# Scoring a sample's cached keys on TensorE from pages the host has laid out in columns

## What is computed

```python
p   = x @ w_in                       # q | k | v | q_m | B | C | h, 2560 columns, for 264 tokens
# prompt: 8 heads of causal attention and 4 heads over 256 memory tokens
# sample b, head h, over its 2048 cached keys in 8 blocks of 256:
gate   = q . mean(k over block)      # one value for each block
chosen = top_k(gate, 3)              # the other five blocks get no weight
logits = q . k / 8 - slope_h * distance
probs  = softmax(logits over the chosen blocks and the token's own key)
o      = probs @ v                   # over the 2048 cached values and the own one
x1  = layernorm(alpha * x + mix(o_attention, o_conv, o_memory) @ w_out)
y   = layernorm(alpha * x1 + moe(x1))   # top 4 of 32 experts, 12.6 MB of weights each
```

## Time and profile before

| | |
|---|---|
| median of 3 runs | 1324.86 us |
| profiled execution, its own time | 1325.73 us |
| its span in the trace | 1323.9 us |
| TensorE busy | 1030.6 us, 78% |
| VectorE busy | 531.0 us, 40% |
| DMA moved | 499.13 MB, mean 377 GB/s |
| chain that ended last | DMA 43%, PE 39%, DVE 6% |

### The profile page before, as it was taken

One profiled execution on the slowest core, in us unless ns is written; L12 is line 12 of the kernel. 1 busy time (PEld: TensorE's weight loads), 2 busy tenths in 40 slices (PEclk: granted clock), 3 DMA queues, 4 the chain that ended last, 5 costly groups with the idle time before them and its releaser, 6 DMA issues.

```text
span 1323.9 us, 20019 instructions
## 1 busy us (share of the span) xinstructions
PE 1030.6 (78%) x7278; PEld 399.6 (30%) x7279; DVE 531.0 (40%) x953; ACT 228.9 (17%) x504; POOL 152.3 (12%) x136
## 2 busy tenths in 40 slices
PE   7998678977985999855556659975778975868956
PEld 5776343433231333211012113221212321222313
DVE  1699884358432444421112123422414441223414
ACT  1212451222111112100010111110111110101112
POOL 2576722205200000000000000000000000000000
PEclk9999678987998999987677779987989997979978
DMA  9986998988999938899999999799999799999993
GB/s 364 398 315 254 358 366 299 391 367 327 370 422 422 422 123 340 346 423 422 423 421 423 421 423 422 318 422 421 423 421 422 318 420 423 421 423 421 423 422 123
DMA packets 72404, 499.13 MB, mean 377 GB/s; under 512 B 7357, under 2 KB 7930, under 8 KB 19034
## 3 DMA queue, kind: packets, MB, share of 16 engines
q1 hardware_dynamic: 66336, 429.88, 79.0%
q0 software_dynamic: 4688, 67.26, 12.6%
q10 hardware_dynamic: 1354, 1.65, 0.3%
HBM read 496.06 MB, written 2.71 MB: 377 GB/s over the span
## 4 chain that ended last, share of the span: by engine, by line
DMA 43%; PE 39%; DVE 6%; issue 4%; POOL 3%; SPq 3%; ACT 1%; ACTq 0%; DVEq 0%; POOLq 0%
DMA gate_up_w<-in_w_gate_up 28%; PE bank L921 14%; DMA down_w<-in_w_down 11%; PE bank L970 10%; PE bank L577 2%; PE bank L705 2%; PE bank L982 2%; DVE down_w L1552 2%; PE bank L794 2%; SPq L505 1%; DMA ring_b<-in_cache_v,page_row 1%; DMA ring_b<-in_cache_k,page_row 1%; PE bank L893 1%; DMA ring_a<-in_cache_k,page_row 1%; POOL ring_b L1487 1%
## 5 line engine op out<-in xcount | busy, mean ns | idle before, releaser
L921 PE MATMUL bank<-gate_up_w,ring_b 128*32 128x512 f32 x3264 | 449.1, 657 | 207.8 <-DMA gate_up_w<-in_w_gate_up 207.7
L1897 DVE TENSOR_TENSOR ring_b<-bank,work 32x512 f32<-32x512 f32 x100 | 68.4, 684 | 486.4 <-ACT work L1268 484.8
L921 PEld LDWEIGHTS bank<-gate_up_w,ring_b 128*32 128x32 f32 x3264 | 89.3, 114 | 454.2 <-DMA gate_up_w<-in_w_gate_up 303.9
L970 PE MATMUL bank<-down_w,ring_b 128*32 128x512 f32 x1632 | 190.2, 598 | 16.9 <-DMA down_w<-in_w_down 16.9
L1494 POOL TENSOR_TENSOR gate_up_w<-gate_up_w,ring_a 128x1024 f32<-128x1024 f32 x1 | 2.3, 2344 | 973.8 <-ACT gate_up_w L1314 973.8
L1268 ACT ACTIVATE work<-bank 32x512 f32<-32x512 f32 x100 | 58.8, 588 | 242.1 <-PE bank L970 240.8
L970 PEld LDWEIGHTS bank<-down_w,ring_b 128*32 128x32 f32 x1632 | 51.2, 111 | 152.1 <-issue 115.8
L1922 DVE TENSOR_SCALAR ring_b<-bank 128x256 f32<-128x256 f32 x51 | 21.7, 425 | 158.3 <-PE bank L921 158.3
L1262 ACT ACTIVATE ring_b<-bank 128x256 f32<-128x256 f32 x51 | 19.5, 383 | 348.0 <-PE bank L947 348.0
L577 PE MATMUL bank<-x_cols,gate_up_w 128*128 128x264 f32 x256 | 61.9, 404 | 0.6 <-ACT x_cols L1106 0.6
L577 PEld LDWEIGHTS bank<-x_cols,gate_up_w 128*128 128x128 f32 x256 | 50.5, 199 | 13.3 <-ACT down_w L1106 2.3
(11 more groups left out here) (370 smaller groups left out, 1029.0 us busy)
## 6 DMA issues: line engine op xcount, KB each, us to landing
gate_up_w<-in_w_gate_up SPq DMA_DIRECT2D x256, 1024.0 KB, 15.1
down_w<-in_w_down SPq DMA_DIRECT2D x128, 1024.0 KB, 11.9
gate_up_w<-in_w_in SPq DMA_DIRECT2D x4, 2048.0 KB, 18.6
gate_up_w<-in_w_out SPq DMA_DIRECT2D x1, 4096.0 KB, 20.7
ring_a<-in_w_in SPq DMA_DIRECT2D x1, 2048.0 KB, 25.8
ring_a<-in_w_mem_kv SPq DMA_DIRECT2D x1, 2048.0 KB, 27.8
down_w<-in_cache_mem_v SPq DMA_DIRECT2D x1, 2048.0 KB, 15.9
x_rows<-in_x_prompt SPq DMA_DIRECT2D x1, 1024.0 KB
```

Of the source, the lines that this page charges most:

```text
L921: last = pe.matmul(p_gu[side][g * SLOTS:(g + 1) * SLOTS, :], xg_t[:, k % 4, k // 4, side * SLOTS:(side + 1) * SLOTS], gate_up_w[:, k, :].r ...
L970: last = pe.matmul(p_down[at_row:at_row + SLOTS, :], hid_t[:, r, k, :], down_rows[:, k, r, h * HALF:(h + 1) * HALF], start=(k == 0), stop= ...
L1897: dve.tensor_tensor(quad_rows[block * SLOTS:(block + 1) * SLOTS, h * HALF:(h + 1) * HALF], bank[1][h * PAIR:h * PAIR + SLOTS, :], down_par ...
```

## The change

The host turns the cache of keys, page by page, into columns: a page is 128 rows of 2 KB, of which row (head parity, dimension) holds four pairs of heads times 128 positions. x and the memory tokens come turned as well. `xt` and `mt` tiles, `spread`, `multiply`, `reduce` and `multiply_back` go. `score_keys(b)` scores a sample with 16 products of 128x32 by 128x512: for each of four pairs of heads, four groups of positions go to four groups of 32 output partitions. Four samples share one bank of PSUM, since `q_diag` is zero outside of a sample's own 8 columns. Pages are fetched one by one, 9 by SyncE (page number into a register, then a DMA) and 7 by GpSimd. The scores lie on 128 partitions (32 sample rows by 4 parts); block choice, softmax and its turning stand between the units, each part of a row has a maximum of its own, and the parts are put together by factors in `row_scale`, applied when the values are masked.

```diff
-        tiles = ([("small", i) for i in range(3)] + [("xt", k) for k in range(KC)] + [("proj", CQ + j) for j in range(4)] +
-                 [("qs", 0)] + [("proj", CC + j) for j in range(4)] + [("mt", k) for k in range(KC)] +
+        tiles = ([("small", i) for i in range(3)] + [("proj", CQ + j) for j in range(4)] +
+                 [("proj", CC + j) for j in range(4)] + [("qs", 0)] +
                  [("mkv", j) for j in range(4)] + [("proj", CK + j) for j in range(8)] +
                  [("proj", CM + j) for j in range(4)] + [("qms", 0)] +
                  [("kr", 0), ("kr", 1), ("vr", 0), ("vr", 1), ("ks", 0), ("vs", 0), ("mr", 0), ("mr", 1)])
         tile_no = {t: i for i, t in enumerate(tiles)}
 
-        SPREAD_AFTER = {("qs", 0): (0, 1), ("mkv", 0): (2,), ("mkv", 3): (3,), ("proj", CK + 2): (4,), ("proj", CV): (5,),
-                        ("proj", CV + 2): (6,), ("proj", CB): (7,)}
+        SCORED_AFTER = {("mkv", 3): 0, ("proj", CK + 1): 1, ("proj", CK + 3): 2, ("proj", CV + 1): 3, ("proj", CV + 3): 4,
+                        ("proj", CM + 1): 5, ("proj", CB + 1): 6}
...
+        def ring_of(b):
+
+            return (b + 1) % 2
+
+        SP_PAGES, POOL_PAGES = range(0, 9), range(9, PAGES)
+
+        def ring_total(b, part):
+
+            return 16 * (b // 2 + 1) + (16 * len(POOL_PAGES) * NS // 2 if part == 0 else 0)
+
+        KEY_BANK = [bank[6], bank[7]]
...
+            def load_keys(b, pages):
+
+                if b:
+                    if b == 1:
+                        sp.wait_ge(tile_ready, tile_no[("mkv", 3)] + 1)
+                    else:
+                        sp.wait_ge(keys_scored, b - 1)
+                for g in pages:
+                    at_page = sp.value_load(page_all[0:1, b * PAGES + g:b * PAGES + g + 1], min_val=0, max_val=NPHYS - 1)
+                    sp.dma_start(ring[ring_of(b)][:, g * AW:(g + 1) * AW],
+                                 cache_k[bass.ds(at_page, 1)].rearrange("a p n -> (a p) n")).then_inc(keys_in[ring_of(b)], 16)
...
+            sp.dma_start(page_all, page_table.rearrange("b g -> (b g)")[None, :].broadcast_to([PARTS, NS * PAGES]))\
+              .then_inc(pages_in, 16)
+            sp.dma_start(x_cols.rearrange("p k t -> p (k t)"), x_turned).then_inc(x_in, 16)
...
-            sp.dma_start(mem_rows, mem_prompt[0].rearrange("(c p) d -> p c d", p=PARTS)).then_inc(mem_in, 16)
+            sp.dma_start(mem_x.rearrange("p k t -> p (k t)"), mem_prompt).then_inc(w_mem_in, 16)
             sp.dma_start(w_mem, w_mem_kv[0].rearrange("(k p) n -> p k n", p=PARTS)).then_inc(w_mem_in, 16)
-            sp.wait_ge(ring_in[1][1], 16)
+            sp.wait_ge(pages_in, 32)
+            load_keys(0, SP_PAGES)
             sp.dma_start(w_in_a[:, :, 512:1024], w_in_k[:, :, 512:1024]).then_inc(w_k_in, 16)
+            load_keys(1, SP_PAGES)
             sp.dma_start(w_in_a[:, :, 1024:1536], w_in_k[:, :, 1024:1536]).then_inc(w_v_in, 16)
+            load_keys(2, SP_PAGES)
             sp.dma_start(w_in_a[:, :, 1536:2048], w_in_k[:, :, 1536:2048]).then_inc(w_m_in, 16)
+            for b in range(3, NS):
+                load_keys(b, SP_PAGES)
...
-            sp.wait_ge(ring_in[1][1], keys_total(NS - 1))
-            sp.wait_ge(back_multiplied, 2 * 4)
             sp.dma_start(w_o, w_out[0].rearrange("(j p) n -> p j n", p=PARTS)).then_inc(w_out_in, 16)
-            sp.wait_ge(back_multiplied, 2 * 5)
+            sp.wait_ge(keys_scored, NS)
             sp.dma_start(ln1_gain, ln1_g[0][None, :].broadcast_to([PARTS, D])).then_inc(ln1_in, 16)
             sp.dma_start(ln1_bias, ln1_b[0][None, :].broadcast_to([PARTS, D])).then_inc(ln1_in, 16)
+            sp.dma_start(x_rows[:, 0:2, :], x_prompt[0].rearrange("(c p) d -> p c d", p=PARTS)).then_inc(x_in, 16)
+            sp.dma_start(x_rows[0:NS, 2, :], x_sample[:, 0, :]).then_inc(x_in, 16)
...
-            sp.wait_ge(ptt_ready, 1)
+            sp.wait_ge(rows_scaled, 1)
...
-            sp.wait_ge(unit_read, 2 * (NS - 1))
-            for part in range(2):
-                sp.wait_ge(ring_in[(NS - 1) % 2][part], ring_total(NS - 1))
-            sp.dma_start(ln2_gain, ln2_g[0][None, :].broadcast_to([PARTS, D])).then_inc(ln2_in, 16)
-            sp.dma_start(ln2_bias, ln2_b[0][None, :].broadcast_to([PARTS, D])).then_inc(ln2_in, 16)
             sp.wait_ge(pieces_ready, 3)
...
+            sp.dma_start(ln2_gain, ln2_g[0][None, :].broadcast_to([PARTS, D])).then_inc(ln2_in, 16)
+            sp.dma_start(ln2_bias, ln2_b[0][None, :].broadcast_to([PARTS, D])).then_inc(ln2_in, 16)
             load_down(*range(at_scores // (2 * D), DK))
...
+            def score_keys(b):
+
+                if b == 0:
+                    pe.wait_ge(query_placed, 1)
+                pe.wait_ge(keys_in[ring_of(b)], keys_total(b))
+                pe.wait_ge(ring_in[ring_of(b)][0], pool_keys_total(b))
+                pages = ring[ring_of(b)].rearrange("p (g c t n) -> p c t g n", g=PAGES, c=4, t=4)
+                for c in range(4):
+                    for t in range(4):
+                        last = pe.matmul(KEY_BANK[b // 4][32 * t:32 * t + 32, :], q_diag[c][:, b, :], pages[:, c, t],
+                                         start=(b % 4 == 0 and c == 0), stop=(b % 4 == 3 and c == 3))
+                last.then_inc(keys_scored, 1)
...
-                for b in SPREAD_AFTER.get((kind, n), ()):
-                    copied(("qs", 0))
-                    spread(b)
+                if (kind, n) in SCORED_AFTER:
+                    score_keys(SCORED_AFTER[kind, n])
...
             for i in range(NU + 2):
                 if i + 1 < NU:
                     unit_scores(i + 1)
-                if i == 2:
-                    pe.wait_ge(so_ready, 1)
-                    pe.matmul(bank[3][0:ROWS, 0:1], so_spread, ones[0:NS, 0:1], start=True, stop=True).then_inc(own_ready, 1)
-                if i == 9:
-                    turn_scores()
+                if i == LAST_KEYS_AT:
+                    spread_own()
+                    score_keys(NS - 1)
+                if i == LAST_KEYS_AT + 2:
+                    sum_gates()
+                if i == LAST_KEYS_AT + 3:
+                    spread_penalty()
+                if i == LAST_KEYS_AT + 5:
+                    turn_exps()
...
-            pe.wait_ge(sm_p, 1)
-            for g in range(PAGES):
-                last = pe.transpose(bank[2 + g // 8][:, (g % 8) * ROWS:(g % 8 + 1) * ROWS],
-                                    logits[:, g * PARTS:(g + 1) * PARTS], ident[0:ROWS, 0:ROWS])
-            last.then_inc(ptt_ready, 1)
-            pe.matmul(bank[5][0:NS, 320:320 + ROWS], po_spread, ident[0:ROWS, 0:ROWS], start=True, stop=True)\
-                .then_inc(po_ready, 1)
+            turn_parts()
...
+            def sample_exps():
+
+                act.wait_ge(sm_max, 1)
+                for u in range(2):
+                    act.activation(logits[:, u, :], logits[:, u, :], ACT.Exp, bias=neg_part_max[:, u:u + 1],
+                                   accum_out=part_sum[:, u:u + 1]).then_inc(sm_exp, 1)
+                act.activation(own_exp, own_exp, ACT.Exp).then_inc(sm_exp, 1)
+
+            def keep_turned_exps():
+
+                for u in range(2):
+                    act.wait_ge(ptt_ready, u + 1)
+                    act.activation(scores.rearrange("p (j t) r -> p j t r", j=4)[:, :, :, 32 * u:32 * u + 32],
+                                   TURNED_BANK[u][:, :].rearrange("p (j t r) -> p j t r", j=4, t=4), ACT.Copy)\
+                       .then_inc(ptt_copied, 1)
+
             for i in range(NU + 2):
+                if i == LAST_KEYS_AT + 5:
+                    sample_exps()
+                if i == LAST_KEYS_AT + 6:
+                    keep_turned_exps()
...
+            rows_k = cache_k.rearrange("n p f -> (n p) f")
+
+            def load_keys(b):
+
+                if b == 1:
+                    pool.wait_ge(tile_ready, tile_no[("mkv", 3)] + 1)
+                elif b:
+                    pool.wait_ge(keys_scored, b - 1)
+                for g in POOL_PAGES:
+                    pool.indirect_dma_start(ring[ring_of(b)][:, g * AW:(g + 1) * AW], None, rows_k,
+                                            bass.IndirectOffsetOnAxis(ap=page_at[:, b * PAGES + g:b * PAGES + g + 1], axis=0),
+                                            bounds_check=NPHYS * PARTS - 1).then_inc(ring_in[ring_of(b)][0], 16)
...
+            pool.wait_ge(page_at_ready, 1)
+            load_keys(0)
...
+            for b in range(1, NS):
+                load_keys(b)
+            pool.wait_ge(tile_copied, tile_no[("proj", CB + 1)] + 1)
+            iota(key_places, [[PARTS, PAGES], [4, 4], [PAGES, PARTS // PAGES]], base=-PAST).then_inc(consts_made, 1)
+            for part in range(2):
+                load_values(0, part)
+            for part in range(2):
+                load_values(1, part)
...
+            def place_queries():
+
+                dve.wait_ge(tile_copied, tile_no[("proj", CQ + 3)] + 1)
```

(61 more changed lines are left out.)

416 lines of the change are left out of this document (173 added, 243 removed).

## The result

The changed kernel takes 1371.82 us (median; 1369.52 to 1386.0), the kernel before 1324.59 beside it: a ratio of **1.038** [1.031, 1.045], slower. The forecast was 1333 with a range from 1315 to 1347. A repeat in another session gave 1.037 [1.034, 1.039]. Four executions of the later runs (one of a4, one of a9, two of the kernel before) took 1558 to 2566 us, far outside of all the others, and the times and ratios here leave them out.

The account below looks back on a forecast made before the run. The expert weight stream was taken as the bound, its start held by projections, units, page values and table. `out_proj` 2.3 us later plus 6 for early tiles gave 8.3 later: 1333.2 against the median 1324.86, range 1315 to 1347.

Parts of the forecast that it names:

- The units: Units stage after the projections: 43.1 - 4 + 3.6 + 2.5 + 5 = 50 us, ending at 196 against 184.85.
- (a): Rival: page traffic beats 387 GB/s, units start at 141; 3 to 4 us faster, or 1317 to 1322; chance 0.24.
- (f): Rival: DMAs wait for each other's completion, nine pages up to 22 us a sample; 1400 and more; chance 0.01.
- (d): Rival: pages cost more than their bytes, 2 to 3 us per sample more; 1340 to 1350; chance 0.12.
- four signs of being wrong: Units starting before 141 or lasting under 45 us, sets not 3.6 us, last values landing within 17 us of issue.
- Projections: Stage before the units: `mkv` ends at about 58.8, units start at 146 against 128.6, bounds 141 and 156.
- these 13 us: Projections: TensorE waits some 13 us for key pages in the first three sets, as traffic at 387 GB/s sets the pace.
- Units besides the stores: Units to page values: units from 146 to 196, then 4 us more, page values at 200.
- To `out_proj`: Page values to first `out_proj`: from 200 to 217.8, making `out_proj` 2.3 us later than before.
- the leg: Path to `out_proj` through the memory keys, landing 8 us after the last unit's end at 195.3, then VectorE's 14.5 us.
- Early tiles: Three expert weight tiles, 3.1 MB, now issued beside the last values delay them 6 us, bounds 0 and 7.4.
- (e): Rival: sets stream slower, at twice the length 7.3 us each, units at about 165; 1350; chance 0.03.

Follow-up runs that it names:

- a4: Changed kernel with the value and memory-query pieces of `w_in` issued ahead of sample 1's key pages on SyncE: 1358.9 us, ratio 1.0284.
- a9: a5 with the tiles that read `ring_a` ahead of the query tiles, their weights loaded first, key sets placed one tile differently: 1332.2 us, ratio 1.0050.
- a1: Changed kernel with turned probabilities in columns of their own and ScalarE's wait for the six stores removed: 1343.75 us, ratio 1.0144.
- a2: Changed kernel with GpSimd issuing the first sample's values only once the six stores are in: 1345.62 us, ratio 1.0149.
- a6: Changed kernel with SyncE issuing the output weight, and all it issues later, only once the six stores are in: 1352.79 us, ratio 1.0187.
- a8: Changed kernel with both the first values and the output weight held behind the six stores: 1347.1 us, ratio 1.0176.
- b1: Kernel before with turned probabilities in columns of their own and no ScalarE wait for the stores: 1326.1 us against 1325.9, ratio 0.9997.
- a3: Changed kernel with SyncE issuing the three early expert weight tiles only after the last sample's values are in: 1366.21 us, ratio 1.0313.
- a10: a9 with key sets of samples 1 to 6 put back and GpSimd issuing sample 1's pages before the scaled identities: 1330.18 us, ratio 1.0031.
- a5: Changed kernel with the edits of a1, a3 and a4 together: 1325.91 us against 1325.89 for the kernel before, ratio 1.0013.

## Why the prediction was wrong

- **The step that failed** is "The units", with its sum of 50 us. It counted what TensorE, VectorE and ScalarE have to do, and added only sample 7's late data. It left out that ScalarE waits there for its own six stores, 22.06 us of TensorE's time. It took the 13.1 us of TensorE's wait for VectorE out of the units as a pure gain; but they were also the time in which the stores landed: from the first store's issue to ScalarE's first copy there were 17.6 us, and now there are 7.8. The stores are issued when the last projection is copied, so they moved 24 us later with the units, past the issue of the first values and of the output weight, which hang on the projections and the key sets; before, both had been issued after the stores (136.5 and 154.4 against 128.6 us). I had used the turns by packet for the early tiles and seen the mix of 16 KB and 2 KB rows for sample 7's pages, but had not gone through ScalarE's queue with it. None of the rivals (a) to (f) has it, and none has 1371.8 us: (d) ends at 1350 and (f) begins at 1400. Of the four signs of being wrong that the prediction names, none came (units began after 141 and lasted over 45 us, a set takes 3.64, the last values need 23.29): all four look at terms that it had. a1, a2, a6, a8 and b1 show the cause.
- **Projections, 6 us short** (units at 152.22, forecast 146). The first weight piece is in at 1.72 + 13.16 = 14.9, 2 us late (10.9 to landing in the earlier trace rows); `mkv` ends at 60.3, not 58.8. The waits for pages were called at 13 us and are 5.37 + 6.52 + 1.12 = 13.0, in the sets of samples 1, 2 and 5. A set takes 3.64 us as said, but after its two long waits TensorE's granted clock is 0.63 and 0.60, and these sets take 5.9 and 6.3, 4.9 more together: a term that the sum lacked.
- **That these 13 us are the price of traffic** was half right. Pages move 378 GB/s from 62 to 146 us (387 said), and nine pages take SyncE some 9.2 us (9.9 said). But the forecast took the third weight piece's standing behind sample 1's pages as given; a4 shows that this order costs 11 us, more than the pages' waits there have.
- **Units besides the stores**: 231.51 - 152.22 - 22.06 = 57.2 us to the page values, forecast 54.
- **To `out_proj`**: 19.1 us from the page values, forecast 17.8; the memory keys are waited for (3.58 us on VectorE), as the leg had it.
- **Early tiles**: +6 said, 23.29 - 16.87 = 6.4 in the chain, 7.0 by a3. Right.
- **The rest**: up to `out_proj` the forecast had +2.3 and the traces have +35.15: of the 32.85 between them 22.06 are the stores, 6.2 the front, 3.2 the units and 1.3 the way to `out_proj`. Of the 43.8 in all, 35.15 and 6.4 are told above; the other 2.2 come behind the last values (41.85 us later than before) ahead of the gathering of rows for the first expert (349.62 against 305.34, 44.28 later), and no run looks at them.
- Rival (a) had the front as fast as a4's 141, but not in the change as it stands. (e) and (f) are excluded: the sets take 3.64 us, and pages overlap.

## What to carry to other kernels

When work moves later, list every DMA that is issued behind it, and for each the wait that it ends, even where that wait costs nothing now: a store that is always in when it is asked for becomes the critical path when two bulk loads get ahead of it. When a wait is taken away, look for what else was done in its time. Small-row stores should be issued, and land, before loads of large rows start on other queues, or else what they are read from should not be reused soon. In a queue that stops for a buffer, nothing should stand behind the stop that doesn't need that buffer.

## What was not expected of the hardware

- Queues share the DMA engines by packets: three have 144, 144 and 144 in 7 us, for 70, 20 and 11% of the time, and two have 513 and 503 in another 7.
- 1.6 MB of stores take 6 us with their queue nearly alone, 15 beside the output weight or the values, and 37 beside both (and the 2 MB that SyncE issues at 168.6), while the traffic there is 419 GB/s.
- A wait of 5 to 6 us on TensorE was followed by a set that took 2.3 to 2.6 us more, at a granted clock of 0.6.
- In a10 TensorE idles less than in a5 from 60 to 75 us (14.54 against 10.78 us busy) and is granted 0.67 instead of 0.88 from 150 to 200. Why the clock is lower there stays open; no run varies it alone, and two executions of the changed kernel differ as much (0.91 and 0.72 from 193 to 226).
